# FFN activations of a four-layer network: turned by VectorE blocks and a scratch in HBM, not by TensorE

## The reference

```python
def swiglu(x, w_gate, w_up, w_down):          # first stack
    return (jax.nn.silu(x @ w_gate) * (x @ w_up)) @ w_down

def swiglu_ffn(x, w_in, w_out):               # second stack
    a, b = jnp.split(x @ w_in, 2, axis=-1)
    return (jax.nn.silu(a) * b) @ w_out

# first stack, each layer:
x = x + 0.5 * swiglu(rmsnorm(x, ffn1_norm[l]), ...)
h = rmsnorm(x, mix_norm[l]); x = x + hybrid_mixer(h, ...)
x = x + 0.5 * swiglu(rmsnorm(x, ffn2_norm[l]), ...)
# second stack, each layer: FFN, mixer, cross attention, FFN, each with layer_norm(ALPHA * x + ...)
```

## Time and profile before

| | |
|---|---|
| median of 3 runs | 2505.05 us (2505.01 to 2505.12) |
| profiled execution, first to last instruction (span) | 2503.6 us |
| TensorE matmuls busy | 2470.2 us, 99% |
| VectorE busy | 1509.2 us, 60% |
| ScalarE busy | 1184.6 us, 47% |
| GpSimd busy | 70.4 us, 3% |
| granted TensorE clock, mean | 0.999 of full speed |
| mean DMA rate | 183 GB/s |

### The profile page before, as it was taken

One profiled execution on the slowest core, in us unless ns is written; L12 is line 12 of the kernel. 1 busy time (PEld: TensorE's weight loads), 2 busy tenths in 40 slices (PEclk: granted clock), 3 DMA queues, 4 the chain that ended last, 5 costly groups with the idle time before them and its releaser, 6 DMA issues.

```text
span 2503.6 us, 31120 instructions
## 1 busy us (share of the span) xinstructions
PE 2470.2 (99%) x13042; PEld 2107.5 (84%) x13042; DVE 1509.2 (60%) x1533; ACT 1184.6 (47%) x1276; POOL 70.4 (3%) x116
## 2 busy tenths in 40 slices
PE   8999999999999999999999999999999999999998
PEld 6889998888888988888889878888888898788887
DVE  6546775555556775555557757755655567577554
ACT  5436444434436444434435664544344355645442
POOL 0000100000000100000000000000000000000000
PEclk9999999999999999999999999999999999999999
DMA  7545445455454445456554445464554544454542
GB/s 303 185 185 189 148 162 207 170 189 206 168 199 182 146 164 202 168 202 203 220 182 178 151 149 214 170 218 168 198 206 168 198 169 154 151 202 162 216 167 101
DMA packets 68195, 458.30 MB, mean 183 GB/s; under 512 B 7752, under 2 KB 9928, under 8 KB 15832
## 3 DMA queue, kind: packets, MB, share of 16 engines
q1 hardware_dynamic: 61488, 433.23, 47.0%
q0 software_dynamic: 4352, 20.45, 2.3%
q10 hardware_dynamic: 2216, 2.63, 0.5%
HBM read 453.65 MB, written 2.62 MB: 182 GB/s over the span
## 4 chain that ended last, share of the span: by engine, by line
PE 91%; DVE 4%; ACT 3%; issue 1%; DMA 1%; SPq 0%; POOL 0%; DVEq 0%; POOLq 0%; ACTq 0%
PE acc L594 24%; PE acc L596 24%; PE acc L595 24%; PE acc L562 4%; PE acc L564 4%; PE acc L563 4%; PE aux L666 2%; DVE w_lo L495 1%; PE aux L793 1%; ACT w_hi L487 1%; DMA raw<-in_w 1%; ACT tmp L1476 1%; PE stat L610 1%; PE bc L610 0%; PE aux L1164 0%
## 5 line engine op out<-in xcount | busy, mean ns | idle before, releaser
L495 DVE TENSOR_TENSOR w_lo<-raw,w_hi 128x2048 fp32r<-128x2048 f32 (+1 forms) x417 | 936.2, 2248 | 784.0 <-ACT w_hi L487 781.0
L487 ACT ACTIVATE w_hi<-raw 128x2048 fp32r<-128x2048 f32 (+1 forms) x417 | 782.9, 1880 | 635.7 <-PE acc L596 608.8
L594 PE MATMUL acc<-w_hi,x_hi 128*128 128x512 f32 (+1 forms) x1848 | 724.8, 392 | 4.3 <-DVE x_lo L1728 2.1
L596 PE MATMUL acc<-w_lo,x_hi 128*128 128x512 f32 (+1 forms) x1848 | 716.8, 388 | 0.0
L595 PE MATMUL acc<-w_hi,x_lo 128*128 128x512 f32 (+1 forms) x1848 | 716.1, 388 | 0.0
L594 PEld LDWEIGHTS acc<-w_hi,x_hi 128*128 128x128 f32 x1848 | 347.6, 188 | 77.9 <-issue 6.1
L596 PEld LDWEIGHTS acc<-w_lo,x_hi 128*128 128x128 f32 x1848 | 347.3, 188 | 72.2
L595 PEld LDWEIGHTS acc<-w_hi,x_lo 128*128 128x128 f32 x1848 | 347.7, 188 | 69.4 <-issue 1.0
L594 PE MATMUL acc<-w_hi,h_parts 128*128 128x512 f32 x704 | 275.4, 391 | 0.0
L596 PE MATMUL acc<-w_lo,h_parts 128*128 128x512 f32 x704 | 274.1, 389 | 0.0
L595 PE MATMUL acc<-w_hi,h_parts 128*128 128x512 f32 x704 | 273.9, 389 | 0.0
(11 more groups left out here) (394 smaller groups left out, 2196.5 us busy)
## 6 DMA issues: line engine op xcount, KB each, us to landing
raw<-in_w SPq DMA_DIRECT2D x399, 1024.0 KB, 4.8
raw<-in_w SPq DMA_DIRECT2D x18, 512.0 KB, 3.3
tmp<-in_norm_gb POOLq DMA_DIRECT2D x8, 1024.0 KB, 5.2
tmp<-in_norm_gb POOLq DMA_DIRECT2D x6, 512.0 KB, 3.9
tmp<-in_gate_rows POOLq DMA_DIRECT2D x12, 256.0 KB, 3.0
gates<-in_mixc POOLq DMA_DIRECT2D x2, 800.0 KB, 5.3
raw<-in_w SPq DMA_DIRECT2D x2, 800.0 KB, 4.5
skew<-tmp ACTq DMA_DIRECT2D x1, 1536.0 KB
```

The lines of the kernel that those rows point to most:

```text
L487: nc.scalar.activation(w_hi[:, slot, 0:kind], raw[:, slot, 0:kind], ACT.Copy).then_inc(hi_done, 1)
L495: nc.vector.tensor_tensor(w_lo[:, slot, 0:kind], raw[:, slot, 0:kind], w_hi[:, slot, 0:kind].bitcast(F32), ALU.subtract).then_inc(lo_done, 1)
L594: nc.tensor.matmul(out, vh, wh, start=first and k == 0, stop=False)
L596: last = nc.tensor.matmul(out, vh, wl, start=False, stop=last_k and k == nk - 1)
```

## The change

TensorE's `turn` is removed. In its place:

- **VectorE** turns `HID` in 32x32 blocks, `turn_squares(i)`: two transposes (128x512, or 128x256 in the sixth block) right behind `times(i, 1)` and ahead of the split of chunk c0+4i+7. They write the tile `SQ`.
- **GpSimd** runs `permute(f, i)` for each block: it stores `SQ` (512 KB) to a scratch in HBM, waits until the store has landed, and issues four transfers that read it back into the tile `HF`, each for 32 partitions, in pieces of 1 KB (512 B in the sixth block). This puts the 32x32 blocks in their places.
- **ScalarE's `hid_high` and VectorE's `hid_low`** stand where they stood, but read `HF` in SBUF instead of `aux` in PSUM, and `hid_high` waits until all four reads have landed (`hid_landed`).
- The rows of the down matrix are permuted on the host (`turned_rows`) to the order that this gives. The size of the loads stays.
- The wait for the constants moves from `turn` to `x_turn`.

```diff
@@ TensorE
-                def turn(i):
-
-                    for tt in range(2):
-                        n = 12 * f + 2 * i + tt
-                        pe.wait_ge(hid_ready, n + 1)
-                        if n == 0:
-                            pe.wait_ge(consts_loaded, 16 * N_CONSTS)
-                        if n >= 2:
-                            pe.wait_ge(hid_parts, n - 1)
-                        for q in range(4 if i < 5 else 2):
-                            last = nc.tensor.transpose(aux[:, tt, q * P:(q + 1) * P], HID[:, tt, q * P:(q + 1) * P], ident[:, :])
-                        last.then_inc(hid_turned, 1)
...
-                    if j % 4 == 0 and j:
-                        turn(j // 4 - 1)
...
-                    if j == 0:
-                        turn(5)
@@ ScalarE
                 def hid_high(i):
+                    w = tiles_of(i)
+                    act.wait_ge(hid_landed, 64 * (6 * f + i + 1))
                     for tt in range(2):
-                        act.wait_ge(hid_turned, 12 * f + 2 * i + tt + 1)
-                        w = 4 if i < 5 else 2
-                        nc.scalar.activation(h_hi[:, 4 * i:4 * i + w, tt * P:(tt + 1) * P],
-                                             aux[:, tt, 0:w * P].rearrange("p (a b) -> p a b", b=P), ACT.Copy).then_inc(hid_hi, 1)
+                        nc.scalar.activation(h_hi[:, 4 * i:4 * i + w, tt * P:(tt + 1) * P].rearrange("p k (a j) -> p k a j", j=32),
+                                             landed(i, tt), ACT.Copy).then_inc(hid_hi, 1)
@@ VectorE
+                def turn_squares(i):
+                    w = tiles_of(i)
+                    n = 6 * f + i
+                    if n:
+                        dve.wait_ge(squares_stored[(n - 1) % 2], 16 * ((n - 1) // 2 + 1))
+                    for tt in range(2):
+                        V_.transpose(SQ[:, 0:w * S].rearrange("p (b t c) -> p b t c", b=4, t=2)[:, :, tt],
+                                     HID[:, tt, 0:w * P].rearrange("p (b c) -> p b c", b=4)).then_inc(squares_ready, 1)
...
                     times(i, 0)
                     times(i, 1)
+                    turn_squares(i)
                     ahead.to(c0 + 4 * i + (7 if i < 5 else 5))
@@ GpSimd
+            def permute(f, i):
+
+                n, w = 6 * f + i, tiles_of(i)
+                pool.wait_ge(squares_ready, 2 * (n + 1))
+                to = squares[n % 2, :, 0:w * S]
+                pool.dma_start(to, SQ[:, 0:w * S]).then_inc(squares_stored[n % 2], 16)
+                pool.wait_ge(squares_stored[n % 2], 16 * (n // 2 + 1))
+                if n:
+                    pool.wait_ge(hid_parts, 2 * n)
+                for b in range(4):
+                    src = to[:, b * w * 64:(b + 1) * w * 64].rearrange("(a r) c -> r a c", a=4)
+                    pool.dma_start(HF[32 * b:32 * b + 32, 0:w * S].rearrange("r (a c) -> r a c", a=4), src).then_inc(hid_landed, 16)
...
+                    for i in range(6):
+                        permute(subs[:s].count("ffn"), i)
```

More of the change, by code:

```diff
@@ L65, in rows_of, with turned_rows @@
     return w.reshape(n, P, -1).transpose(1, 0, 2).reshape(1, P, -1)
+def turned_rows(w):
+    n = w.shape[0] // P
+    return rows_of(w.reshape(4, n, 32, -1).transpose(1, 0, 2, 3).reshape(w.shape))
 def moving(w):
@@ L83, in ffn_weights @@
         for j in range(5):
-            out[WIDE].append(rows_of(w[512 * j:512 * j + 512]))
-        out[HALF].append(rows_of(w[2560:]))
+            out[WIDE].append(turned_rows(w[512 * j:512 * j + 512]))
+        out[HALF].append(turned_rows(w[2560:]))
 def pack(i):
@@ L344, in program @@
         first_loaded, first_hi, first_lo = sem("first_loaded"), sem("first_hi"), sem("first_lo")
-        silu_ready, hid_ready, hid_turned, hid_hi, hid_parts = (
-            sem(n) for n in ("silu_ready", "hid_ready", "hid_turned", "hid_hi", "hid_parts"))
+        silu_ready, hid_ready, squares_ready, hid_hi, hid_parts = (
+            sem(n) for n in ("silu_ready", "hid_ready", "squares_ready", "hid_hi", "hid_parts"))
+        squares_stored = [sem(f"squares_stored{i}") for i in range(2)]
+        hid_landed = sem("hid_landed")
         v_chain, a_chain, g_chain = (sem(n) for n in ("v_chain", "a_chain", "g_chain"))
@@ L376, in program, with flat @@
         e.update({n: sem(n) for n in names3})
+        def flat(ap):
+            return ap.rearrange("p a b -> p (a b)")
         GB = tmp[:, 28:36].rearrange("p a b -> p (a b)")
@@ L386, in program @@
         HID = tmp[:, 20:24].rearrange("p (t a) b -> p t (a b)", t=2)
+        SQ = flat(tmp[:, 24:28])
+        HF = flat(tmp[:, 8:12])
+        squares = nc.dram_tensor("squares", (2, P, 4 * S), F32, kind="Internal").ap()
         BIAS = tmp[:, 0:8]
@@ L443, in program, with tiles_of @@
         JUNK1 = QT[:, 0]
-        def flat(ap):
-            return ap.rearrange("p a b -> p (a b)")
         def ps(tile):
             return acc[:, tile % RING, :]
+        def tiles_of(i):
+            return 4 if i < 5 else 2
         def split_at(ap, li):
@@ L460, in packed, with landed @@
             return ap[:, 0:S].rearrange("p (g b) -> p g b", b=b)
+        def landed(i, tt):
+            w = tiles_of(i)
+            v = HF[:, 0:w * S].rearrange("p (a t k j) -> p a t k j", a=4, t=2, j=32)
+            return v[:, :, tt].rearrange("p a k j -> p k a j")
         def ended(eng, tile):
@@ L599, in x_turn @@
             def x_turn(N, tt):
+                if N == 1 and tt == 0:
+                    pe.wait_ge(consts_loaded, 16 * N_CONSTS)
                 if N == 7 and tt == 0:
@@ L1800, in times @@
                     if n >= 2:
-                        dve.wait_ge(hid_turned, n - 1)
+                        dve.wait_ge(squares_ready, n - 1)
                     if s == 0:
@@ L1808, in times @@
                     dve.sem_inc(acc_taken[tile % RING], 1)
+                def turn_squares(i):
+                    w = tiles_of(i)
+                    n = 6 * f + i
[4 more added lines that the diff above has]
+                                     HID[:, tt, 0:w * P].rearrange("p (b c) -> p b c", b=4)).then_inc(squares_ready, 1)
                 def hid_low(i):
+                    w = tiles_of(i)
                     for tt in range(2):
                         dve.wait_ge(hid_hi, 12 * f + 2 * i + tt + 1)
[L1813 to L1816, removed]
+                        to, hi = (v[:, 4 * i:4 * i + w, tt * P:(tt + 1) * P].rearrange("p k (a j) -> p k a j", j=32)
+                                  for v in (h_lo, h_hi))
+                        V_.tensor_tensor(to, landed(i, tt), hi.bitcast(F32), ALU.subtract).then_inc(hid_parts, 1)
                 if s == 0:
@@ L1822, in ffn @@
                 times(0, 1)
+                turn_squares(0)
                 ahead.to(c0 + 7)
```

## The result

The changed kernel takes 2602.84 us (median of 4 runs, 2600.19 to 2604.39) against 2505.03 before (median of 4 as well): a ratio of 1.039, 95% interval 1.0377 to 1.0402. It is 98 us slower. Forecast were 2465.5 us, with a range up to 2545; the result lies outside, on the side of the third case, which had a chance of 0.23.

A forecast was written before the change was run, and what follows sets the result against it. TensorE's matmuls, busy 99% of the span, were taken as the bound. Span 2503.6 us less 39.5 for removed transposes, all else hidden, plus 1.45 of run above span gave 2465.5 us, range 2459 to 2545.

The forecast's parts named there:

- the third case: D above 13.0: ScalarE waits at `hid_landed` with weight splits due behind it, every block; 2552 to 2672 us; chance 0.23.
- TensorE sheds: Removing the transposes from TensorE's list saves 4.94 us an FFN, 39.5 us over eight.
- held at a third read: GpSimd's third read might be held 2.40 us at issue, as in earlier transfers, making D 11.5 us.
- lands 3.0 us after that if it is as quick as 256 KB: 4.6 us: Four reads of 128 KB: last issued 1.6 us after the first, landing 3.0 us later, 4.6 us together.
- I take 9.1 to 11.5 as likeliest: The expected D in us: 9.1 from the parts' low values, 11.5 with the third and fourth read held.
- D: Delay from the end of VectorE's pair of transposes to the landing of the fourth read; likeliest 9.1 to 11.5 us.
- 12.9 and 16.5: D in us with held reads plus weight loads sharing the DMA engines; 16.5, with an 8.0 us last read, is the upper end.
- The arithmetic of the margin: How late the reads may land in an FFN's blocks before TensorE loses time: D up to 12.2 us is hidden.
- the 20.8 us: Latest harmless landing, counted from B, before TensorE's matmul lacks `w_lo` of chunk 4i+9.
- B: Start of the ScalarE split that a block's last chunk releases; without `turn` it returns every 21.8 us.

The follow-up runs named there:

- e1: Changed kernel without the store and four reads; ScalarE and VectorE split the tile of the 32x32 transposes directly: 2464.77 us.
- e3: Changed kernel with ScalarE's and VectorE's split of a block moved behind the weight splits of the next block: 2464.54 us.
- e11: Changed kernel with SP holding back two weight loads of each full block until that block's reads have landed: 2478.92 us.
- e5: Changed kernel with only the first block of each FFN split late, blocks 1 to 5 as they were: 2492.68 us.
- e2: Changed kernel with one read of 128 whole rows in place of the four, blocks not put in their places: 2507.08 us.
- e4: Changed kernel with the blocks put in place by four stores, then one read of 128 whole rows: 2531.71 us.
- e8: Changed kernel with each of the four reads bringing 32 whole rows, blocks not put in their places: 2576.99 us, one run.
- e10: Changed kernel with each of the four reads taking all 128 rows of a quarter of the columns: 2528.67 us, one run.
- e6: Built on e1, without store and reads; ScalarE's split waits for five 32 KB loads issued one after another: 2675.91 us.
- e7: Built on e1, without store and reads; ScalarE's split waits for seven 32 KB loads issued one after another: 2876.66 us.

## Why the forecast was wrong

**What held.** TensorE sheds 40.6 us by e1, forecast 39.5. The pair of transposes takes 1.31 us, as 1.3 were taken, and is hidden. So is the split from SBUF, the moved wait and, by e3, the whole traffic: e1 and e3 run in 2464.8 and 2464.5 us, where the sum of the forecast said 2465.5. GpSimd was not held at a third read, so half of what the third case rested on did not occur.

**The step that failed** is the term "lands 3.0 us after that if it is as quick as 256 KB: 4.6 us" for the four reads, and with it "I take 9.1 to 11.5 as likeliest". Measured are 11.2 us for the four reads in the block read above, 6.9 for the median one, and D of 13.2 to 17.0 in blocks 0 to 3 (the fifth FFN left out, see below). The other parts of D were near: 4.4 us to the first read against 4.5, and 3.9 to 6.4 in other blocks. The forecast allowed for weight loads beside the reads, but only on top of a held third read (12.9 and 16.5), and it put the third case at 0.23 because that "needs both the hold and contention at once". Contention alone was enough. By an estimate from the figures of the Trainium skill (DMA: Bandwidth & Descriptors, Anatomy of one DMA) the store was to take 3.2 us and a read 2.3. For a read with no weight load beside it (e11, 2.9 us) the trace agrees with the page to 0.6 us; for one beside two of them (changed kernel, 6.9 us) it does not. The store takes 2.9 us in e3 and 3.9 in the changed kernel, both with a load beside it for a part of the time.

**What the term left out** are the neighbours that the reads would have. The durations were taken from transfers of a program whose splits come every 5.44 us. In block 0 this was wrong from the start: two weight loads are in flight there even in e3 and e5, where ScalarE does not wait for that block, and the four reads take 8.8 to 11.2 us. In the blocks behind it there is a feedback. A late landing lets ScalarE do several splits in one go, VectorE then does two in a row behind its transposes, and SP issues two loads of 1 MB 2.2 us apart where one stood in e3. The loads of `raw` issued from 595 to 640 land in 4.7, 6.1 and 10.7 us (least, median, most), and the reads among them are late again. That this circle exists is shown from three sides. e3 takes ScalarE's wait away, and the four reads of a block fall from 10.0 to 5.9 us where one load stands in place of two. e5 moves block 0 alone, and in the third FFN D of the two blocks behind it falls by 6.0 and 5.0 us. e11 leaves all waits of the engines and moves loads only, and D falls to 8 to 10 in this FFN. Which DMA engines the slow reads stand in, and behind which packets, the runs do not show.

**The arithmetic of the margin nearly held.** The forecast let six D come to 6 x 12.2 = 73 us before anything is lost. The sum of D less the waits is 70.5 in the changed kernel, 64.2 in e2, 70.0 in e4, 69.7 in e8, 66.9 in e10, 73.9 in e6 and 80.0 in e7. Two of its parts were off, in opposite directions. The next pair of transposes ends 11.4 us behind a late landing (631.82 - 620.39), not 10.9. And it erred on who waits first. That is not the matmul that needs `w_lo` (the 20.8 us) but the one that needs a bank: it is due 5.44 us earlier, when TensorE begins the next block, and starts 1.8 us behind the landing (649.19 - 647.41), so the landing may be at B + 19.7 at most (21.8 - 0.3 - 1.8). Of the 94.4 us of waits in the changed kernel, 94.0 are for silu.

**A term was missing.** The changed kernel's span is 135.4 us above e1's. 94.4 of it are TensorE's idle time (127.1 - 32.7); the other 41.0 are TensorE's busy time for the same list (2471.3 - 2430.3), at a granted clock of 0.980. The Trainium skill (TensorE: Matmul & The Clock Gate, Part 1: The HAM clock gate) has an idle TensorE fall back to half its clock, and the trace agrees: 0.50 in 648 to 654, behind the wait of 4.97 us. The third case priced waits alone. For the measured sum of D it would give (82.3 - 73.2 - 4.94) x 8 = 33 us above before. The profiled executions are 94.8 us apart (2598.4 - 2503.6). Of the 62 us between, 41 are the slower clock and 22 the margin, which was 70.5 us in the place of 73.2 (8 x 2.7); 1 us less comes from what TensorE shed (40.6 against 39.5).

## What to carry to other kernels

A latency costs by what stands behind its landing in program order. The same transfers cost nothing when the consumer was placed behind the more urgent weight splits (e3, 2464.5 us, 1.6% faster than before), and 138 us when it stood ahead of them. Price a transfer with the neighbours that it will have after the change: the four reads took 4.6 us with no weight load in flight (e11), 5.9 with one (e3) and 10.0 with two (changed kernel). Then ask whether its lateness bunches them; where a delay returns once per block, a few us of error are multiplied by the number of blocks, and an engine that had to wait comes back at a lower clock.

## What the runs showed that was not expected

- The same read of 128 KB takes 2.9 us (e11), 4.2 (e3) or 6.9 (changed), by the weight loads beside it, although the DMA engines move only 194 GB/s on the mean in the changed kernel.
- In the fifth FFN the first read of block 2 follows its transposes only after 16.8 to 19.5 us in place of some 4, in e3, e5, e11 and the changed kernel alike, because the store lands so late. In the changed kernel:

```profile
1250.38 2.21 POOL L2475 DMA_DIRECT2D tmp<-squares  x4 [16.85 <-DMA squares<-tmp]
```

ScalarE sends its bias rows to HBM there (`bias_copy`, in sublayer 6, 1.5 MB). It is not the store that makes this place slow. e6 has no store, and one of its 32 KB loads takes 12.7 us there in place of 2.1; its successor waits for it:

```profile
1285.11 0.53 POOL L2481 DMA_DIRECT2D tmp<-in_ident  x1 [12.48 <-DMA tmp<-in_ident]
```

And in the kernel before, the four weight loads issued from 1176 to 1191, just behind the bias transfer (1170.39), land in 13.1 to 18.0 us in place of 4.8 (median 16.7):

```profile
raw<-in_w SPq DMA_DIRECT2D x4, 1024.0 KB, 16.7
```

So the place was slow before the change, for the loads of another queue too, and hid it. That the bias transfer is the cause fits all of these traces, but no run left it out. The place gives e11 its only wait for a silu, and e3 hides even this. With the store cut in four (e4), the first read there follows the transposes after 17.8 us, no sooner.
- A TensorE wait is dearer than its length: in the changed kernel 94.4 us of idle time came with 41.0 us of slower matmuls, from e6 to e7 156.5 came with 46.7.
